# The rows of x as the starting value of the four output quarters in a two-product MLP

## The reference, cut to what matters

```python
x = x + g1 * (mix @ w_out)
h = rms_norm(x, norm2_g) * (1.0 + sc2) + sh2
x = x + g2 * (jnp.square(jax.nn.relu(h @ w_ff1)) @ w_ff2)   # w_ff1: 1024 x 4096, w_ff2: 4096 x 1024
```

## Time and profile before

| | us |
|---|---|
| median of 3 runs (2303.45 to 2309.29) | 2306.15 |
| the profiled execution | 2303.62 |
| its span, first to last instruction | 2301.7 |
| TensorE (PE) busy | 2207.7 (96%) |
| VectorE (DVE) busy | 1846.1 (80%) |
| ScalarE (ACT) busy | 1121.8 (49%) |
| GpSimd (POOL) busy | 358.6 (16%) |

### The profile page before, as it was taken

How to read it: one execution, slowest core, us unless ns; L and a number is a source line. 1 busy time by engine, 2 the same in 40 slices (tenths; PEclk the granted TensorE clock), 3 DMA queues, 4 the chain that set the end, 5 groups by cost and what they waited for, 6 DMA issues and landing times. The chain is left out here.

```text
span 2301.7 us, 29815 instructions
## 1 busy us (share of the span) xinstructions
PE 2207.7 (96%) x11258; PEld 1853.9 (81%) x11258; DVE 1846.1 (80%) x2593; ACT 1121.8 (49%) x1787; POOL 358.6 (16%) x285
## 2 busy tenths in 40 slices
PE   7999999987999999999999999998999999999998
PEld 4988897866889888878888788887887888878887
DVE  6548796989989886788888998877687777898887
ACT  4532554448888864433334545443343333545452
POOL 0343043833455640000000000000000000000000
PEclk9999999989999999999999999999999999999999
DMA  7441435130000035268888543447234444743434
GB/s 270 160 160 47 147 119 165 37 106 28 15 15 24 10 125 178 88 224 290 280 282 305 184 169 133 173 152 250 101 119 143 154 154 155 255 161 137 169 137 174
DMA packets 185738, 345.10 MB, mean 150 GB/s; under 512 B 11496, under 2 KB 83452, under 8 KB 184572
## 3 DMA queue, kind: packets, MB, share of 16 engines
q1 hardware_dynamic: 185508, 343.16, 43.9%
q10 hardware_dynamic: 88, 0.04, 0.0%
HBM read 236.20 MB, written 106.95 MB: 149 GB/s over the span
## 5 line engine op out<-in xcount | busy, mean ns | idle before, releaser
L2952 PE MATMUL ps<-sb_h_hi 128*128 128x512 f32 x512 | 200.1, 391 | 7.9 <-ACT ps L1710 2.6
L2954 PE MATMUL ps<-sb_h_hi,sb_h_lo 128*128 128x512 f32 x512 | 199.3, 389 | 0.0
L2953 PE MATMUL ps<-sb_h_lo,sb_h_hi 128*128 128x512 f32 x512 | 199.2, 389 | 0.0
L2918 PE MATMUL ps<-sb_h_hi,sb_w_hi 128*128 128x512 f32 x448 | 176.8, 395 | 9.1 <-DVE sb_u_full L2425 9.0
L2601 PE MATMUL ps<-sb_h_hi,sb_w_hi 128*128 128x512 f32 x448 | 177.4, 396 | 0.7 <-DVE sb_w_lo L2235 0.7
L2919 PE MATMUL ps<-sb_h_lo,sb_w_hi 128*128 128x512 f32 x448 | 175.4, 392 | 0.0
L2603 PE MATMUL ps<-sb_h_hi,sb_w_lo 128*128 128x512 f32 x448 | 174.5, 389 | 0.0
L2602 PE MATMUL ps<-sb_h_lo,sb_w_hi 128*128 128x512 f32 x448 | 174.4, 389 | 0.0
L2116 DVE TENSOR_SCALAR_CACHE_REDUCE sb_scores<-ps 128x1024 f32<-128x1024 f32 (+7 forms) x160 | 139.6, 891 | 12.4 <-PE ps L2815 6.9
L2952 PE MATMUL ps<-sb_w_hi 128*128 128x512 f32 x384 | 149.4, 389 | 0.0
L2953 PE MATMUL ps<-sb_w_lo,sb_w_hi 128*128 128x512 f32 x384 | 149.4, 389 | 0.0
(11 more groups left out here) (342 smaller groups left out, 5924.3 us busy)
## 6 DMA issues: line engine op xcount, KB each, us to landing
left_scratch<-sb_u_sum SPq DMA_DIRECT2D x128, 256.0 KB, 5.9
sb_right<-w_gated_scratch SPq DMA_DIRECT2D x16, 2048.0 KB, 8.7
sb_h_lo_full<-left_scratch SPq DMA_DIRECT2D x64, 512.0 KB, 3.8
sb_w_full<-in_w_ff SPq DMA_DIRECT2D x28, 1024.0 KB, 6.3
left_scratch<-sb_u_full SPq DMA_DIRECT2D x96, 256.0 KB, 2.3
sb_w_full<-left_scratch SPq DMA_DIRECT2D x48, 512.0 KB, 3.3
sb_w_raw<-in_w_in SPq DMA_DIRECT2D x16, 1024.0 KB, 6.0
sb_ada<-in_w_ada SPq DMA_DIRECT2D x32, 512.0 KB, 5.3
```

What stands on the lines that cost most here:

```text
L2918: M(psum[:, bank, :], wh[:, k, :], rh[:, k, :], start=fresh and k == 0, stop=False, skip_group_check=True)
L2952: M(dst, hi[:, k, tok], hi[:, 2 + k, :], start=fresh and k == 0, stop=False, skip_group_check=True)
L2953: M(dst, hi[:, k, tok], low[:, 2 + k, :], start=False, stop=False, skip_group_check=True)
L2954: ins = M(dst, low[:, k, tok], hi[:, 2 + k, :], start=False, stop=k == 1, skip_group_check=True)
```

## The change

The rows of x_mid are loaded into `out11`, `out12`, `out22`, `out21` while the first product ends and in chunk 0 (`load_mid`, 1 MB each), and chunk 0 adds to them instead of copying over them. After the last chunk these tiles are the output and are stored by quarters. The row additions of the last chunk go; two additions per side bring in `part5`. The splits for the next pass stand between the evacuations. The rows of x for the second pass lie in `x_second`, apart from the output tiles. Part 3 of w_out is used ahead of part 2 in the first tile of the second pass. In the first fast group, `sum22` comes ahead of the splits; in all fast groups, `fold(0, g)` stands behind the second bank sum instead of ahead of `sum22`.

```diff
@@ -74,6 +74,7 @@
+WO_ORDER = (0, 1, 3, 2)
 FOLDS = FAST - 1
@@ -323,8 +324,7 @@
 part5 = [sb(f"part5{p}", k, [P, 2, BLK]) for p, k in enumerate((196, 0.5))]
-x_pair = [sb(f"x_pair{p}", 144 + 8 * p, [P, 2, D]) for p in range(3)]
-x_one = [sb(f"x_one{p}", k, [P, 1, D]) for p, k in enumerate((168, 200))]
+x_second = [sb(f"x_second{t}", k, [P, D]) for t, k in enumerate((144, 148, 152, 156, 160, 164, 168, 200))]
 w_full = [sb(f"w_full{s}", 86 + 16 * s, [P, ITEM]) for s in range(4)]
@@ -387,13 +387,13 @@
     "ff1_mm", "relu_ready", "sq_ready", "sum_ready")]
-out_st = [sem(f"out_st{p}") for p in range(HT // 2)]
+out_st = {s: sem(f"out_st{s}") for s in (1, 3, 4, 6)}
 u00_st, u10_st, u11_st, sum_st, sum4_st = [sem(n) for n in ("u00_st", "u10_st", "u11_st", "sum_st", "sum4_st")]
...
     "slot_hi", "slot_lo", "part_mm", "part_copied", "part_read")]
-x_mid_st, x_late_ld = sem("x_mid_st"), [w_second_ld, w_third_ld, lam_ld, ada0_ld[SLOTS]]
-upper_done, folded = sem("upper_done"), sem("folded")
+x_mid_st, x_mid_ld = sem("x_mid_st"), {1: w_second_ld, 3: w_third_ld, 4: lam_ld, 6: ada0_ld[SLOTS]}
+folded = sem("folded")
 fold_ld, fold_st = x_ld, qk_ld
@@ -546,7 +546,7 @@
 def wo_no(hc, i):
-    return 2 * NI + hc * KC_OUT + i
+    return 2 * NI + hc * KC_OUT + (WO_ORDER.index(i) if hc else i)
@@ -559,12 +559,18 @@
-def x_late(e):
-    return x_pair[e // 2][:, e % 2, :] if e < 6 else x_one[e - 6][:, 0, :]
 def x_rows(hc, t):
-    return x_late(t) if hc else x_new[:, t, :]
+    return x_second[t][:, :] if hc else x_new[:, t, :]
+def quarter_sum(s):
+    return {1: out11, 3: out12, 4: out22, 6: out21}[s]
+def quarter_rows(view, hc, s, t0, n):
+    a, b = {1: (0, 0), 3: (1, 0), 4: (1, 1), 6: (0, 1)}[s]
+    r = hc * HT + 4 * b + t0
+    return view[:, r:r + n, a * BLK:(a + 1) * BLK]
@@ -854,8 +860,8 @@
             sp.wait_ge(xr_ld, 16 * n)
-        if hc:
-            sp.wait_ge(out_st[t // 2], 32)
+        if hc and t == 0:
+            sp.wait_ge(slot_lo, 2 * SLOTS * CHUNKS)
         sp.dma_start(x_rows(hc, t), x_v[:, n, :]).then_inc(xr_ld, 16)
@@ -904,12 +910,12 @@
-    def load_late(hc, e):
-        sp.dma_start(x_late(e), x_mid_v[:, hc * HT + e, :]).then_inc(x_late_ld[e // 2], 16)
-    def store_out(hc, e):
-        sp.wait_ge(part_read, read_no(hc, CHUNKS - 1, 3 if e < 4 else 6, e % 4 // 2))
-        sp.dma_start(out_v[:, hc * HT + e, :], x_late(e)).then_inc(out_st[e // 2], 16)
+    def load_mid(hc, s):
+        sp.dma_start(quarter_sum(s)[:, :, :], quarter_rows(x_mid_v, hc, s, 0, 4)).then_inc(x_mid_ld[s], 16)
+    def store_out(hc, s, t0, n):
+        sp.wait_ge(part_read, read_no(hc, CHUNKS - 1, s, (t0 + n - 1) // 2))
+        sp.dma_start(quarter_rows(out_v, hc, s, t0, n), quarter_sum(s)[:, t0:t0 + n, :]).then_inc(out_st[s], 16)
@@ -938,7 +944,7 @@
                 if hc:
-                    sp.wait_ge(part_read, read_no(0, CHUNKS - 1, 6, 1))
+                    sp.wait_ge(out_st[6], 32)
                 sp.dma_start(by_k8(w1_first[hc][:, :]), w_ff1_v[:, :, 0:GW]).then_inc(w1p_ld, 16)
@@ -1003,6 +1009,8 @@
             load_left(hc, 0, s)
+        for s in (1, 3, 4):
+            load_mid(hc, s)
         store_left_sums(hc, FG - 1)
@@ -1022,11 +1030,14 @@
                 load_left(hc, ch + 1, s)
+                if ch == 0 and s == 2:
+                    for stored in (u00_st, u10_st, u11_st):
+                        sp.wait_ge(stored, 16 * (group_no(hc, FG - 1) + 1))
+                    sp.wait_ge(sum_ready, 4 * (group_no(hc, FG - 1) + 1))
+                    load_mid(hc, 6)
         G = chunk_no(hc, CHUNKS - 1)
-        sp.wait_ge(slot_lo, 2 * SLOTS * (G + 1))
-        for e in range(HT):
-            load_late(hc, e)
         if hc == 0:
+            load_rows(1, 0)
             sp.wait_ge(part_mm, part_no(G, 1, 3))
@@ -1035,19 +1046,22 @@
                 load_mix(HT + n)
+        store_out(hc, 1, 0, 4)
+        if hc == 0:
+            load_rows(1, 1)
             sp.wait_ge(part_mm, part_no(G, 3, 3))
             load_w_out(1, 1)
-            sp.wait_ge(upper_done, 1)
+            sp.wait_ge(out_st[1], 16)
             load_w_out(1, 3)
+        store_out(hc, 3, 0, 4)
+        if hc == 0:
             sp.wait_ge(part_mm, part_no(G, 5, 3))
             load_w_out(1, 2)
-        for e in range(HT):
-            store_out(hc, e)
-            if hc == 0 and e == HT // 2 - 1:
-                load_rows(1, 0)
-                load_rows(1, 1)
-    for p in range(HT // 2):
-        sp.wait_ge(out_st[p], 64)
+        store_out(hc, 4, 0, 4)
+        store_out(hc, 6, 0, 2)
+        store_out(hc, 6, 2, 2)
+    for s, n in ((1, 2), (3, 2), (4, 2), (6, 4)):
+        sp.wait_ge(out_st[s], 16 * n)
@@ -1554,6 +1568,8 @@
                 A(w_hi[2][:, :], w1_first[hc][:, :], ACT.Copy).then_inc(w1p_hi, 1)
+            if hc and t == 1:
+                act.wait_ge(out_st[4], 16)
             if t:
@@ -1735,8 +1751,8 @@
             mix_head(HT + 1)
+            wo_head(1, 3, (out_st[3], 16))
             wo_head(1, 2, (part_mm, part_no(G, 5, 3)))
-            wo_head(1, 3, (upper_done, 1))
@@ -2240,6 +2256,8 @@
                 dve.wait_ge(xt_ready, NT + n)
+            if hc and t == 0:
+                dve.wait_ge(out_st[4], 16)
             normalise(NT + n, x_rows(hc, t), xn2[hc][:, :])
@@ -2368,9 +2386,7 @@
-            if s == 5:
-                return part5[p][:, :, :]
-            return {1: out11, 3: out12, 4: out22, 6: out21}[s][:, 2 * p:2 * p + 2, :]
+            return part5[p][:, :, :] if s == 5 else quarter_sum(s)[:, 2 * p:2 * p + 2, :]
@@ -2379,7 +2395,9 @@
             y = sum_of(s, p)
-            if c:
+            if c == 0 and s != 5:
+                dve.wait_ge(x_mid_ld[s], 16 + 16 * (hc + 1))
+            if c or s != 5:
                 ins = V.tensor_tensor(out=y, in0=y, in1=two(side_of(s), p), op=ALU.add)
@@ -2408,28 +2426,31 @@
                 w1_sums(g + 1)
-                for i in range(3):
+                for i in range(0 if g == PLAIN else 3):
                     w1_tail(g + 1, i)
-            dve.wait_ge(fast_relu, 2 * n + 1)
-            square(0, 0)
+            if g > PLAIN:
+                dve.wait_ge(fast_relu, 2 * n + 1)
+                square(0, 0)
             if last:
...
                 right_add(0, 3)
-            else:
+            elif g > PLAIN:
                 for i in range(3, 5):
                     w1_tail(g + 1, i)
-            fold(0, g)
             dve.wait_ge(fast_mm, SLOTS * n + 5)
...
                             op=ALU.add).then_inc(sum22, 1)
+            if g == PLAIN:
+                dve.wait_ge(fast_relu, 2 * n + 1)
+                square(0, 0)
             dve.wait_ge(sum22, n + 1)
...
             else:
-                for i in range(5, SLOTS):
+                for i in range(2) if g == PLAIN else range(5, SLOTS):
                     w1_tail(g + 1, i)
@@ -2438,6 +2459,10 @@
                 tails(0, 1)
+            if g == PLAIN:
+                for i in range(2, SLOTS):
+                    w1_tail(g + 1, i)
+            fold(0, g)
             u_sums(g)
@@ -2528,66 +2553,45 @@
-        def add_to_rows(p, a, y):
-            col = slice(a * BLK, (a + 1) * BLK)
-            dve.wait_ge(x_late_ld[p], 16 + 32 * (hc + 1))
-            if p < 3:
-                rows = x_pair[p][:, :, col]
-                return V.tensor_tensor(out=rows, in0=rows, in1=y, op=ALU.add)
-            for i in range(2):
-                row = x_one[i][:, 0, col]
-                ins = V.tensor_tensor(out=row, in0=row, in1=y[:, i, :], op=ALU.add)
-            return ins
-        def finish(s, p, rows_no, added):
-            dve.wait_ge(part_mm, part_no(chunk_no(hc, c), order_of(c).index(s), 2 * p + 1))
-            dve.wait_ge(dve_chain, added)
-            add_to_rows(rows_no, 1, two(side_of(s), p)).then_inc(part_read, 1)
+        def add_fifth(s, p):
+            y = sum_of(s, p)
+            return mark(V.tensor_tensor(out=y, in0=y, in1=sum_of(5, p), op=ALU.add))
...
         evacuate(c, 1, 1)
-        dve.wait_ge(part_read, read_no(hc, c, 1, 1))
-        add_to_rows(0, 0, sum_of(1, 0))
         evacuate(c, 5, 0)
-        add_to_rows(1, 0, sum_of(1, 1))
         evacuate(c, 5, 1)
-        added = mark(add_to_rows(0, 1, sum_of(3, 0)))
-        add_to_rows(1, 1, sum_of(3, 1)).then_inc(upper_done, 1)
         dve.wait_ge(part_read, read_no(hc, c, 5, 1))
-        dve.wait_ge(dve_chain, added)
-        top = [mark(add_to_rows(0, 1, sum_of(5, 0)))]
-        dve.wait_ge(upper_done, hc + 1)
-        top.append(mark(add_to_rows(1, 1, sum_of(5, 1))))
-        added = mark(add_to_rows(2, 1, sum_of(4, 0)))
-        first = [mark(add_to_rows(2 + p, 0, sum_of(6, p))) for p in range(2)]
-        dve.wait_ge(dve_chain, added)
-        bottom = mark(add_to_rows(2, 1, sum_of(5, 0)))
-        finish(3, 0, 0, top[0])
-        finish(3, 1, 1, top[1])
-        finish(4, 0, 2, bottom)
-        link(add_to_rows(3, 1, sum_of(4, 1)))
-        bottom = mark(add_to_rows(3, 1, sum_of(5, 1)))
```

(34 more changed lines are left out.)

## The result

The changed kernel takes 2314.58 us (median of 7 runs), the kernel before 2306.15: a ratio of 1.0041, 95% interval 1.0028 to 1.0054. It is slower by 0.4%, outside the predicted range of 2286 to 2305. One of the seven executions took 3670.53 us at a mean granted clock of 0.555 and is left out of the ratio; the other six lie between 2311.06 and 2321.26.

The account below looks back on a forecast made before the run. PE, busy 96% of the span, was taken as the bound, so only its idle or slow-clock time could be won. -3.2 + 3.0 + 2.0 - 9.8 - 4.5 + 2.2 - 2.4 = -12.7 us gave 2293 on the median, range 2286 to 2305.

Parts of the forecast that it names:

- Store and load take 7.3: First pass's fold loop: fold store to landed next weights, 7.3 us in a 19.15 us loop, hidden under PE's 19.04.
- upper price of both: If queue order holds, fold store plus weights and the loads ahead of load_right(1) cost their upper bounds, 8.2 and 6 us.
- (a): Rival: the fold loop binds at 20.15 us, total -2.4, giving 2304, no change; chance 0.20.
- (c): Rival: the fold's own load is also late, loop 21.5 us per group, +12.5, giving 2319, slower; chance 0.06.
- Against it: the load's start overlaps: Argument against the 20.15 us loop: part of the weight load's start is hidden under the fold store's data.
- First fast group: Product 6 there no longer stalls in either pass; the second pass gains its stall and slow matmuls, -4.5 us.
- Product 6 of the second group: First pass, second fast group: starts at 1022.5 against 1025.30, -2.8 us, after a stall at product 4.
- Product 6 of the last fold group: End of the first pass's fold loop: small stalls on fold loads vanish, 0.8 kept for jitter, -3.2 us.
- Right matrix of chunk 0: load_right(0) waits for the later last fold store: +3.0 us, stall of 0.68 grows to near 4, slow matmuls covered.
- `load_right(1)`: Chunk 0: three 1 MB loads ahead make the matrix about 3.8 us late, +2.0 and +2.2 us in the two passes.
- Boundary: Between passes: fewer VectorE operations let slot 6 and the second projection start earlier at full clock, -9.8 us.
- End: Last stall goes, -1.0, and SP stores 0.5 MB instead of two such pieces, 1.3 to 1.5 less; -2.4 us.

Follow-up runs that it names:

- 12: Changed kernel with the fold's store cut in two: one row of 0.26 MB ahead of the next weights' load, the rest behind it; 2293.8 us, ratio 0.9949.
- 2: Changed kernel with one swap on SP: the fold's store issued behind the next group's weight load, the fold itself still late; 2288.9 us, ratio 0.9928.
- kernel 5: Changed kernel with the fold's store issued by ScalarE in its own queue, the weight load still on SP at the same moment; 2300.0 us, ratio 0.9975.
- Kernels 8 to 11: Changed kernel with weight load ahead of fold store, evacuate(c, 4, 0) earlier, third x_mid quarter behind load_right(1), plus variations; 2282.7, 2282.6, 2281.6, 2284.2 us.

## Why the prediction was wrong

**The step that failed** is a term of the loop: "Store and load take 7.3", from "so the two together cost between 6.6 and 8.2". They took 9.1. The rest of that sum held (10.0 for 10.1 us from landing to fold, 1.75 for the fold), so the loop was 20.8 us instead of 19.15 and became the bound. Its upper end was too low, for two reasons that the trace of before held already. The 8.2 of the earlier trace rows is one landing of twelve; they lie between 7.5 and 9.6, 8.5 in the mean. And the 6.1 of a load "alone" was taken with the store issued 2.1 us ahead, which landed 2.0 us into the load; with the store's 0.79 MB straight ahead of it, at the 355 to 400 GB/s of the earlier trace rows, 6.1 + 2.0 to 2.2 + 0.4 is 8.5 to 8.7. What is still missing to 9.1 is the 6.1 itself: the twelve loads of before took 6.3 us in the mean. The sentence on the ring order (the Trainium skill, "DMA: Bandwidth & Descriptors", section on queues, rings and completion order) pointed the same way with its "upper price of both", but that price was the 8.2, and the runs went beyond it. Kernels 12 and 2 fit that rule; kernel 5 shows that the order makes only 0.6 us of the 2.3, and that most of the delay comes even when the store is in another queue.

**The rivals.** What happened is the mechanism of (a) with a size between (a)'s 20.15 and (c)'s 21.5; (c)'s own mechanism, a fold that waits for its load, was not seen in the changed kernel. The prediction's own crossing point, "slower than before by 0.3% from a loop of about 20.9", is close to what was measured: 20.8 and 0.41%. "Against it: the load's start overlaps" did not hold.

**Point by point.**
- *First fast group*: product 6 without idle in both passes, right. Second pass: -4.5 predicted, -4.7 measured.
- *Product 6 of the second group*: predicted 2.8 us earlier, measured 0.2 (1032.76 - 990.25 = 42.5 against 42.7). Again the transfers: the first weights landed 9.7 us after the store, and the stall at product 4 was 4.76.
- *Product 6 of the last fold group*: -3.2 predicted, +15.9 measured (1259.58 - 990.25 = 269.3 against 253.4). This is 19.1 us, the bulk of the error.
- *Right matrix of chunk 0*: +3.0 predicted; product 6 of the last group is another 2.4 us late, with 3.31 us of stall for "near 4". But its slow matmuls, costed at nothing, take 4.4 in place of 2.7 us.
- *`load_right(1)`*: +2.0 and +2.2. By the stall's place in its stage +1.4 (41.0 after the start against 39.6) and +2.2 (41.6 against 39.4). Kernels 8 to 11 show that the x_mid loads ahead of it are the cause.
- *Boundary*: -9.8 predicted. The second product's -2.7 less the 1.1 of the previous point (as left at its second stall) is -3.8, and the projection's -2.5 makes -6.3. The stall of 4.91 and the slow start of the projection went as said. "6.1 us to land" was 7.3, so slot 6 stood for 1.96 us, and its 24 matmuls took 7.16 for 5.44. In kernels 12 and 5, with the same code at the boundary, the load took 6.0 and 5.7 us and slot 6 stood for 0.66 and 0.39: the path was as predicted, and the load's time to land decided, 7.3 for 6.1. It varies from kernel to kernel; what makes it vary was not tried.
- *End*: -1.4 for the stores, measured -1.2; the stall of 0.83 went.

The account closes: the measured stages sum to +9.7. Take away the loop's error of 19.1 (from -3.2 to +15.9) and the boundary's 3.5 (from -9.8 to -6.3), and -12.9 is left, for a predicted -12.7.

## What to carry to other kernels

When an operation moves later, list what SP issues behind its store, and close the loop: landing, work, store, next landing. Add the bytes ahead of a load to its time at the rate that the trace shows, and take the latency from all turns of the loop, not from one. Here the cure was no return to the old order, but one swap in the queue: the load that the loop waits for ahead of the store that nobody waits for.

## What the runs showed of the hardware

A 1 MB load took 6.4 us with the fold's store behind it, 8.7 behind 0.79 MB in the same queue, and 8.1 beside the same 0.79 MB in another engine's queue. A second queue brought back 0.6 us only. And the issue of one 1 MB store on SP, the first output store of the first pass, took 4.4 to 5.7 us in all eleven kernels that have it (5.32 in the changed one, at 1571.29 above), in which SP issued nothing else; the same store in the second pass took 0.4. Ahead of it stand a load of x, one of w_out and two of the mixer's rows, issued within 4 us; whether they are the cause was not tried.
